# A hybrid state-space and attention layer with expert lookup: later fifth modulation quarter, biases off TensorE, one more early gather page, other picks summed by VectorE, output tail in halves

## The reference, cut to what matters

```python
sh1, sc1, g1, sh2, sc2, g2 = split(silu(c) @ w_mod + b_mod, 6)      # w_mod 1024 x 6144
h = rmsnorm(x, norm1) * (1 + sc1) + sh1
u, c_q, c_kv, k_rope = split(h @ w_in)
ssm_out = s5_mixer(u)                 # chunked scan, gelu, gate: y * sigmoid(y @ w_glu)
attn = attend(c_q, c_kv, k_rope)      # 8 heads; the sample also reads a cache of 128 tokens
x = x + g1 * (concat(ssm_out, attn) @ w_out)
h2 = rmsnorm(x, norm2) * (1 + sc2) + sh2
q = (h2 @ w_query).reshape(-1, 8, 2, 128)
s = einsum(q, sub_keys); top_s, top_i = top_k(s, 16)                # each half
best_s, pos = top_k(all 16 * 16 pairs, 16); idx = expert numbers; g = softmax(best_s)
act = gelu(einsum('nd,nhkd->nhk', h2, u_table[idx])) * g            # 8 heads x 16 = 128 experts a token
x = x + g2 * einsum('nhk,nhkd->nd', act, v_table[idx])
y = rmsnorm(x, final_norm)
```

## Time and profile before

| what | value |
|---|---|
| median of 3 runs | 878.6 us (877.61 to 880.52) |
| the profiled execution: its own time | 880.12 us |
| the profiled execution: span | 878.3 us |
| PE busy | 717.9 us (82%) |
| DVE busy | 598.0 us (68%) |
| ACT busy | 336.9 us (38%) |
| POOL busy | 369.5 us (42%) |
| HBM read | 318.97 MB, of which the 256 gathers (queue q0) 268.45 MB |
| mean rate of the DMA engines over the span | 365 GB/s |
| mean granted TensorE clock | 0.973 |

### The profile page before, as it was taken

One profiled execution on the slowest core, in us unless ns is written; L12 is line 12 of the kernel. 1 busy time (PEld: TensorE's weight loads), 2 busy tenths in 40 slices (PEclk: granted clock), 3 DMA queues, 4 the chain that ended last, 5 costly groups with the idle time before them and its releaser, 6 DMA issues. The chain is left out here.

```text
span 878.3 us, 11411 instructions
## 1 busy us (share of the span) xinstructions
PE 717.9 (82%) x3937; PEld 360.7 (41%) x3937; DVE 598.0 (68%) x1284; ACT 336.9 (38%) x984; POOL 369.5 (42%) x335
## 2 busy tenths in 40 slices
PE   3898898999884887999968878786978877788774
PEld 0585664654552436567723322232322322222221
DVE  7979411367589865986897775788678468745554
ACT  3512144135436343453343443334334333433332
POOL 3428800034233543354464544453645444444410
PEclk9999999999997999999998999999999999999999
DMA  9954257659998999999999999999999999999992
GB/s 366 411 207 171 77 189 303 241 207 353 410 406 306 392 422 419 381 423 420 419 421 421 422 420 422 421 421 420 422 422 419 423 422 423 420 421 422 420 423 86
DMA packets 45665, 320.94 MB, mean 365 GB/s; under 512 B 5340, under 2 KB 6044, under 8 KB 7592
## 3 DMA queue, kind: packets, MB, share of 16 engines
q0 software_dynamic: 36864, 268.45, 74.4%
q1 hardware_dynamic: 8376, 51.59, 15.0%
q10 hardware_dynamic: 368, 0.18, 0.1%
HBM read 318.97 MB, written 1.23 MB: 365 GB/s over the span
## 5 line engine op out<-in xcount | busy, mean ns | idle before, releaser
L809 PE MATMUL psum<-mem 128*128 128x512 f32 x928 | 460.0, 627 | 117.0 <-ACT mem L1187 116.4
L1465 POOL DMA_INDIRECT mem<-uv_table,small x256 | 303.1, 1184 | 359.6 <-PE psum L809 215.9
L1806 DVE CUSTOM_DVE_ANT_0 mem<-mem,h 128x1024 f32<-128x1024 f32 x256 | 312.4, 1226 | 180.6 <-DMA mem<-uv_table,small 172.8
L809 PEld LDWEIGHTS psum<-mem 128*128 128x128 f32 x928 | 166.0, 195 | 381.2 <-ACT mem L1187 244.6
L1176 ACT ACTIVATE small<-small 128x1 f32<-128x1 f32 x256 | 51.8, 202 | 319.7 <-DVE small L1806 311.1
L1187 ACT ACTIVATE mem<-consts,small 128x128 f32<-128x128 f32 x232 | 93.2, 402 | 7.6
L1181 ACT ACTIVATE small<-small 128x1 f32<-128x1 f32 x256 | 75.4, 295 | 24.8 <-ACT small L1176 1.9
L756 PEld LDWEIGHTS psum<-hT,mem 128*128 128x128 f32 x480 | 58.6, 196 | 15.8 <-issue 10.0
L756 PE MATMUL psum<-hT,mem 128*128 128x128 f32 x480 | 59.3, 279 | 5.4 <-DMA mem<-w_query 5.4
L1384 POOL TENSOR_SCALAR small<-small 128x1 f32<-128x1 f32 (+1 forms) x9 | 4.1, 453 | 108.3 <-DVE small L1697 58.2
L462 PE MATMUL psum<-mem,scol 128*32 128x512 f32 x128 | 22.0, 770 | 15.8 <-DMA mem<-w_mod 15.8
(11 more groups left out here) (221 smaller groups left out, 673.3 us busy)
## 6 DMA issues: line engine op xcount, KB each, us to landing
mem<-w_mod SPq DMA_DIRECT2D x24, 1024.0 KB, 7.9
mem<-w_query SPq DMA_DIRECT2D x8, 1024.0 KB, 9.7
mem<-w_out SPq DMA_DIRECT2D x4, 1024.0 KB, 7.8
mem<-uv_table,small POOLq DMA_INDIRECT x256, 24.9
mem<-w_in_u SPq DMA_DIRECT2D x2, 1024.0 KB, 14.2
mem<-w_in_qkv SPq DMA_DIRECT2D x2, 1008.0 KB, 11.4
mem<-w_ukv SPq DMA_DIRECT2D x1, 1024.0 KB, 8.4
mem<-w_glu SPq DMA_DIRECT2D x1, 1024.0 KB, 5.1
```

Source lines behind the costliest of these rows:

```text
L809: mm = pe.matmul(bank(f"acc_{g}_{half}"), diag[:, pick % DEEP, :], row_of(pick)[:, D + 512 * half:D + 512 * half + 512], start=first, stop ...
L1465: pool.indirect_dma_start(row_of(pick), None, uv_table, bass.IndirectOffsetOnAxis(ap=idx[:, pick:pick + 1], axis=0)).then_inc(row_landed[R ...
L1806: dve.tensor_tensor_reduce(out=row[:, 0:D], in0=row[:, 0:D], in1=h[:, pick // PICKS, :], scale=1.0, scalar=0.0, op0=ALU.mult, op1=ALU.add, ...
```

## The change

The lists and the row plan: picks 17 to 37 leave ADDED; page 16 stands for `late[:, 0:2048]`, which holds g1 and a temporary of the prompt's residual before, and is used for picks 2 and 7. The page of an ADDED pick is put back in the queue two picks later.

```diff
-    free = [15, 3, 4, 5, 2, 13]
+    free = [15, 3, LATE, 4, 5, 2, 13]
...
-        if pick:
+        if pick - 2 in ADDED:
+            queue.append((rows[pick - 2], pick - 2))
+        if pick and pick not in ADDED and not (page_ == LATE and pick > 2):
             queue.append((page_, pick))
...
-ADDED = [pick for pick in range(96) if pick % 4 == 1]
+ADDED = [pick for pick in range(96) if pick % 4 == 1 and not 16 < pick < 40]
+LATE = 16
```

```diff
-            sp.dma_start(brow[0:12, :], b_mod).then_inc(brow_in, 16)
+            sp.dma_start(brow[0:4, :], b_mod[0:4]).then_inc(brow_in, 16)
...
                 load(PAGES[n][0])
+                if PAGES[n][0] == "mod2a.1":
+                    wait_emptied(sp, "mq1")
+                    for j in range(2):
+                        sp.dma_start(modrow[32 * j + 2:32 * j + 3, 1, :], b_mod[4 + j:5 + j]).then_inc(g1_bias_in, 16)
...
+            wait_emptied(sp, "mq2b")
+            for j in range(2):
+                sp.dma_start(brow[32 * j + 2:32 * j + 3, :], b_mod[10 + j:11 + j]).then_inc(g2_bias_in, 16)
...
-            for g, y in enumerate((y_prompt, y_sample)):
-                sp.wait_ge(y_out_ready, g + 1)
-                sp.dma_start(y, h[:, g, :]).then_inc(stored, 16)
-            sp.wait_ge(stored, 2 * 16)
+            sp.wait_ge(y_out_ready, 1)
+            sp.dma_start(y_prompt, h[:, 0, :]).then_inc(stored, 16)
+            for half in range(2):
+                cut_ = slice(512 * half, 512 * half + 512)
+                sp.wait_ge(y_out_ready, 2 + half)
+                sp.dma_start(y_sample[:, cut_], h[:, 1, cut_]).then_inc(stored, 16)
+            sp.wait_ge(stored, 3 * 16)
```

```diff
-            wait_emptied(pe, "mq1")
+            probs_turned(0, 0)
+            probs_turned(0, 1)
             for half in range(2):
                 spread_row("g1", 0, half)
-            pair_step("a", 0)
-            pair_step("a", 1)
-            probs_turned(0, 0)
-            probs_turned(0, 1)
             pe.wait_ge(yg_ready, 1)
             gate_projection(0, (0, 1, 2, 3))
             attended(0)
             wait_emptied(pe, "at0")
             out_projection(0, 0, range(4, 8), first=True)
             out_projection(0, 1, range(4, 8), first=True)
-            pair_step("a", 2)
-            pair_step("a", 3)
             pe.wait_ge(ssm_ready, 1)
             out_projection(0, 0, range(4), last=True)
+            out_projection(0, 1, range(4), last=True)
+            for i in range(4):
+                pair_step("a", i)
             columns_turned()
-            out_projection(0, 1, range(4), last=True)
-            gate_projection(1, (0, 1, 2, 3))
-            pair_step("b", 0)
             normed_turned(0, 0)
             normed_turned(0, 1)
+            gate_projection(1, (0, 1, 2, 3))
             pe.wait_ge(y_read, NC)
-            latents(1, (0,))
             first_queries()
+            pair_step("b", 0)
             pair_step("b", 1)
             first_scores(0)
             second_queries()
...
             pair_step("b", 3)
-            latents(1, (1, 2, 3, 4, 5, 6, 7))
+            latents(1, range(KD))
```

ACT: `gate_evac(1)` stands behind `root_spread(0)` and `normed_evac(0, 1)`. POOL: gather 2 waits for the prompt's square sum (`sq2_ready`) instead of the sample's latents. DVE: `norm_columns` adds `b2col` where it copied, and stands behind the residual and its square sum. The tail of the sample, on ACT, on POOL, and on DVE (in `add_experts(1)` and in `finish_group(1)`):

```diff
+            for half in range(2):
+                cut_ = slice(512 * half, 512 * half + 512)
+                act.wait_ge(x_out_ready, half + 1)
+                act.activation(squares[:, cut_], x[:, 1, cut_], ACT.Square, accum_out=half_sums[:, half:half + 1]).then_inc(sqf_ready, 1)
...
-            inverse_root(rstd_f[:, 1:2], ms_f[:, 1:2], [(0, 1, D)], sqf_ready, 2, rstdf_ready)
+            pool.wait_ge(sqf_ready, 3)
+            step(pool.tensor_tensor(ms_f[:, 1:2], half_sums[:, 0:1], half_sums[:, 1:2], ALU.add))
+            inverse_root(rstd_f[:, 1:2], ms_f[:, 1:2], [(0, 1, D)], sqf_ready, 3, rstdf_ready)
...
+                else:
+                    dve.wait_ge(fn_in, 16)
+                    tt(out2, x[:, g, :], fnb, ALU.mult)
...
+                else:
+                    for half in range(2):
+                        cut_ = slice(512 * half, 512 * half + 512)
+                        dve.tensor_scalar(h[:, g, cut_], out2[:, cut_], rstd_f[:, 1:2], None, ALU.mult).then_inc(y_out_ready, 1)
```

81 lines of the change are left out of this document (48 added, 33 removed).

## The result

The change made the kernel slower: 891.31 us as the median of 4 runs (891.04 to 894.52), beside 879.56 for the kernel before in the same session, ratio 1.0128 (95% interval 1.0097 to 1.0159; the ratio is estimated from all executions, so it is not quite the quotient of the two medians). In a later session the same kernel stood at 1.0078 (1.0048 to 1.0107). Forecast were 874.0 and a chance of 0.11 for slower. The profiled execution of the change took 894.52 us, its span is 892.7, 14.4 more than before.

A forecast was written before the change was run, and what follows sets the result against it. DMA gathers at 421 GB/s were taken to bound the kernel, leaving time lost before the queue stays full and the tail. Terms -0.6 (A to D), -3.3 (E) and -0.7 (F) sum to -4.6: median 874.0 us, range 868.5 to 881.

The forecast's parts named there:

- A: Second quarter's biases: four small matmuls (1.04 us) leave PE and everything behind moves up; -1.0 us, ends -1.04 and 0.
- B: Probabilities turned first on PE, then g1 spread once two 2 KB DMAs land; 0 us, ends -1.1 and +1.0.
- C: Fifth quarter moved behind the out product: first scores at 178.5 against 174.56 us, +3.9, ends +2.3 and +5.8.
- The rival named this clock: Start delay carried to the end, with 2 us for PE's clock: +5.2, 883.8 us; decided by gather 14; chance 0.12.
- D: Seventh early page gives the late start back by gather 14: net -0.6 us with A and C, ends +3.9 and -3.1.
- After that the rate stays near 421: DMA rate in GB/s after the low windows at 276 to 288 us, which were said to lose 5.4 us.
- the hole only moves: Gather 32 holds the queue just as long in the low-rate windows, so E is -0.5: 876.8 us; chance 0.20.
- E: Picks 17 to 37 summed without DVE shrink the low-rate windows at 276 to 288 us: -3.3, ends 0 and -6.0.
- F: Tail behind the last gather done in halves, square sum to store: -0.7 us, ends +0.2 and -1.4.
- PE's first wait for w_mod: Sign for the forecast: PE waits on DMA for w_mod near 163 us, and again near 176.
- gather 31 was 2.5 us earlier against gather 14: Sign for the forecast: gather 31 starts 2 to 4 us earlier against gather 14.
- gather 14 was 13.6 us late: Sign for the forecast: gather 14 starts by 230 us; over 2 us late would show it wrong.

The follow-up runs named there:

- best2: best1 with the biases of both pairs also taken off PE and no small DMA ahead of g1's spread; ratio 0.9948 to the kernel before.
- b_order: The kernel before with only the new order of PE, ACT and DVE around the out product; ratio 1.0118 to the kernel before.
- a_fix: The change with mod2a.3 loaded into page 12 and normed x in PSUM banks 4 and 5; ratio 1.0065 to the kernel before.
- b_rows: The kernel before with only the seventh page and the new picks (17 to 37 left to PE); ratio 0.9984 to the kernel before.
- b_hot: b_rows with small matmuls adding zero on PE, 16 ahead of pick 25's sum and 8 ahead of pick 26's; ratio 0.9965 to the kernel before.
- best1: The kernel before with seventh page, new picks, tail in halves, and the sample's exponentials later on ACT (behind picks 25 and 27); ratio 0.9949 to the kernel before.
- best3: best2 with small matmuls adding zero ahead of the sums of picks 24, 25, 26 and 28; ratio 0.9969 to the kernel before.

## Why the prediction was wrong, point by point

- **A (biases, -1.0).** Not seen in the front's spread of 126 to 135 us. In best2, where only the pairs' matmuls went and no DMA came in front, 0.8 us came out of the stretch.
- **B (probabilities first, 0).** The step "until about 136.7" let PE wait for DVE for nothing. It waits 4.94 us and goes on at the half clock: transposes 1.97 us for 1.09, g1's spread up to 3.6. From scores to gate it is 11.6 us in the change's first profile, 12.4 in the second and 12.8 in b_order, against 10.7: +0.9 to +2.1, where the upper end was +1.0. That the small DMAs land before PE needs them was right here, and only thanks to this wait.
- **C (+3.9, ends +2.3 to +5.8).** The first failing term. From the end of the out product to the first scores the forecast had 20.1 us, the trace has 26.0. mod2a.3 came as worked out: the last pair step ends 7.1 us behind the product, forecast 7.0. Then the sentence "x is turned and multiplied in 2.0 us" fails: 2.0 us of wait for `norm_columns`, a dependency through the bank plan that the forecast lacks, and 1.5 to 1.7 of half clock. The turned columns cost about 1 us more, the gate 0.9, and a pause of 0.8 without a releaser stands before the queries. The wait for mod2b.1 that was expected near 176 did not come in the change; a_fix has it. The rival named this clock, priced it at 2 us, and decided wrongly: it gave the carrying to gather 14 the deciding role, and 0.12.
- **D (page, -0.6).** The second failing term: the late start was to be given back behind the first scores, and nothing of it was (690.54 and 690.51 us). The direction was right at gather 14: in the old order the page gave 2.5 us there, in the change 1.2. But the term was carried to the end, where page and picks changed 0.4 us (b_rows). The hole takes about 2.2 us of such a head start and the second hole another 1. The second one stands in the trace of the kernel before (344 GB/s in 356 to 364 us), and so does a fourth window of the first (315 GB/s); "After that the rate stays near 421" overlooked both. The rival "the hole only moves" comes nearest to what happened to D and E; where gather 32 met the product the hole also grew.
- **E (-3.3).** "About 2.5 us each at the half clock" was a mean over records at both clocks; one sum at the half clock takes 3.78. And "what is late next is pick 26; nothing of that changes" missed ACT's extra diagonal (0.4 us) and, above all, that DVE, relieved of its sum, reaches its long product 1.2 us earlier, so that gather 32 falls inside it. The hole's loss grew by 2.0 us (b_rows) to 2.2 (the change) instead of shrinking by 3.3; in the second profile of the change, where the gather missed the product by 0.20 us, it was as before. The 3.4 us of the forecast also set the row's release (274.3) against gather 31's start (277.69); against the release it replaces (277.4) they are 3.1.
- **F (tail, -0.7).** Right in sign; 12.8 to 12.9 us in the eleven profiles with the new tail, 13.1 to 13.2 in the five with the old: -0.3. The figure for a store that the prediction takes from the Trainium skill is fitted there to DMAs that GpSimd issues, and this store is issued by SP; no term of the sum uses it.

The sum was -4.6, with about +2.9 at the first scores, -6.8 behind them and -0.7 at the end. Measured were +10.5, 0.0 and -0.4. So of an error of 14.7 us, 7.6 are B and C and 6.8 are D and E: with the order priced rightly, the forecast would still have been 7 us too low. Of the signs that were to show it right, PE's first wait for w_mod came as worked out, and gather 31 was 2.5 us earlier against gather 14, though only in the first of two profiles (1.0 in the second). The others did not come: gather 14 was 13.6 us late, the hole wider, and the rate under 421 GB/s again after 300 us.

## What to carry to other kernels

Before work is moved in a hand-written order, list for each moved step all that it waits for: the load and the queue in which it stands, and also who last used its PSUM bank. A wait put on PE costs its length and then the half clock for the microseconds behind it; here 3.2 + 2.0 + 4.9 us of waits in a path of 46 drew some 3 us of clock with them. Look through the whole trace for windows of a low rate before a head start is carried to the end: here two holes took it away. Only versions that also worked on the hole came clear of the kernel before (b_hot, best1, best2, best3), each with several edits at once. And look at what runs on DVE when POOL issues a gather: one gather that started inside a long product of DVE left the gathers' queue empty for 3 us more, and whether it met the product differed between two executions of the same program.

## What of the hardware was not expected

- Sixteen profiles of programs that are nearly alike up to there reach the attention scores between 126.0 and 134.8 us, two profiles of the same program 3.3 us apart, with pauses of PE that have no releaser. So stretches between fixed points are compared here.
- PE had two rows of 2 KB only 6.2 us after SP had issued them, behind two loads of 1 MB.
- A gather's issue takes 0.94 us; beside DVE's product of two SBUF operands of 128 x 2048 (2.29 us) it took 2.97. This is not one row: of the 256 gathers of the kernel before, 114 start while DVE's dot product (1.23 us) runs, and most of them end 0.81 to 0.89 us behind it, however early they started; most of the 38 that meet no dot product take 0.94 to 1.18 us. The first packet follows the end of the issue by 0.7 us (283.10 in the kernel before, 284.07 in b_rows, 295.68 in the change, 275.93 in b_hot), so the data are late too.
- The Trainium skill (SBUF — State Buffer, Who interferes with whom) has such a product contend with GpSimd's reads, and infers that it does not stall DMAs that GpSimd issues. These rows and packets speak against the inference.
